# Pairs of heads on TensorE and half of the difference on ScalarE in the scan of the last two layers

## The reference, cut to what matters

```python
xbc = silu(causal_depthwise_conv(xbc, conv_w, conv_b))
xs, bm, cm = split(xbc, [1024, 1280])             # x, B and C
dt = softplus(dt_raw + dt_bias)                   # (256, 16)
A = -exp(a_log)                                   # (16,)
a_cs = cumsum(dt * A)                             # falls with t
decay[h, t, s] = exp(a_cs[t, h] - a_cs[s, h])     # for s <= t, else 0
y[t, h] = sum_s (C[t] . B[s]) * decay[h, t, s] * (x * dt)[s, h]   # B, C of the head's group
y = rmsnorm((y + d_skip * x) * silu(z), norm_w)
```

## Time and profile before

| | |
|---|---|
| median of 3 runs | 3577.18 us (3576.35 to 3582.57) |
| the profiled execution | 3575.29 us |
| its span, first to last instruction | 3573.5 us |
| TensorE (PE) busy | 3418.4 us, 96% |
| VectorE (DVE) busy | 1963.5 us, 55% |
| ScalarE (ACT) busy | 549.2 us, 15% |
| GpSimd (POOL) busy | 161.1 us, 5% |
| mean granted TensorE clock | 0.968 of full |

### The profile page before, as it was taken

How to read it: one execution, slowest core, us unless ns; L and a number is a source line. 1 busy time by engine, 2 the same in 40 slices (tenths; PEclk the granted TensorE clock), 3 DMA queues, 4 the chain that set the end, 5 groups by cost and what they waited for, 6 DMA issues and landing times. The chain is left out here.

```text
span 3573.5 us, 54659 instructions
## 1 busy us (share of the span) xinstructions
PE 3418.4 (96%) x23594; PEld 2873.7 (80%) x23594; DVE 1963.5 (55%) x2748; ACT 549.2 (15%) x1032; POOL 161.1 (5%) x166
## 2 busy tenths in 40 slices
PE   6999999997899989999899999999899999999999
PEld 2445475545788879998799999999888988889988
DVE  2266762225666746661566666644466665374772
ACT  1100011223343421001100000000101123101130
POOL 0000002000000010000000000000032000060000
PEclk7999999998889999999999999999999999999999
DMA  8887823102323244444344444455444433434423
GB/s 343 311 343 313 314 103 124 59 12 65 94 71 86 50 182 154 172 177 154 118 167 173 165 164 166 174 180 186 154 142 150 157 107 118 153 142 154 157 80 130
DMA packets 134896, 559.63 MB, mean 157 GB/s; under 512 B 57552, under 2 KB 61904, under 8 KB 72256
## 3 DMA queue, kind: packets, MB, share of 16 engines
q1 hardware_dynamic: 120256, 456.17, 36.3%
q10 hardware_dynamic: 14448, 100.62, 7.1%
HBM read 539.25 MB, written 17.30 MB: 156 GB/s over the span
## 5 line engine op out<-in xcount | busy, mean ns | idle before, releaser
L470 PE MATMUL ps<-arena,ring 128*128 128x256 f32 (+2 forms) x3168 | 829.6, 425 | 27.6 <-issue 11.8
L470 PEld LDWEIGHTS ps<-arena,ring 128*128 128x128 f32 x3168 | 609.0, 193 | 246.5 <-issue 172.6
L2586 PE MATMUL ps<-arena 128*128 128x128 f32 x2560 | 292.4, 275 | 0.0
L2586 PEld LDWEIGHTS ps<-arena 128*128 128x128 f32 x2560 | 289.1, 192 | 0.0
L2586 PE MATMUL ps<-arena,ring 128*128 128x128 f32 x1920 | 220.9, 275 | 0.0
L2586 PEld LDWEIGHTS ps<-arena,ring 128*128 128x128 f32 x1920 | 217.7, 192 | 0.1
L2992 PE MATMUL ps<-arena 128*128 128x128 f32 x1792 | 204.7, 275 | 0.0
L2992 PEld LDWEIGHTS ps<-arena 128*128 128x128 f32 x1792 | 202.4, 192 | 0.0
L801 DVE SCALAR_TENSOR_TENSOR arena<-arena,small 128x512 f32<-128x512 f32 x240 | 180.5, 752 | 37.3 <-DMA arena<-in_ada_late 21.3
L3545 PE MATMUL ps<-arena,ring 128*128 128x256 f32 x832 | 180.3, 379 | 0.0
L3545 PEld LDWEIGHTS ps<-arena,ring 128*128 128x128 f32 x832 | 157.9, 190 | 22.4 <-issue 1.0
(11 more groups left out here) (509 smaller groups left out, 4397.5 us busy)
## 6 DMA issues: line engine op xcount, KB each, us to landing
ring<-in_weights SPq DMA_DIRECT2D x402, 1024.0 KB, 4.8
arena<-in_ada_late ACTq DMA_DIRECT2D x64, 1024.0 KB, 8.9
arena<-in_gates SPq DMA_DIRECT2D x56, 256.0 KB, 3.5
arena<-in_front ACTq DMA_DIRECT2D x8, 1024.0 KB, 9.0
arena<-in_x ACTq DMA_DIRECT2D x2, 2048.0 KB, 12.7
keep_g<-arena SPq DMA_DIRECT2D x14, 256.0 KB, 2.0
arena<-keep_h SPq DMA_DIRECT2D x3, 1024.0 KB, 6.4
arena<-in_ctx ACTq DMA_DIRECT2D x1, 2048.0 KB, 23.8
```

The costliest lines, as they stand in the source:

```text
L470: mm = M.matmul(o, ring[:, slot, k, c0:c0 + w], rhs, start=(kc == 0), stop=(kc == ktiles * WK - 1))
L2586: mm = M.matmul(o, w[:, k], x(k), start=(k == 0), stop=(k == HD - 1))
```

## The change

The scan of both layers is done in another order and with another split of the work:

- Difference: VectorE makes only the first 256 columns, as max(sum - acs, 0), in one instruction, and no longer waits for its own end. The other 128 columns are made by ScalarE as Relu(sum - acs) (`later_half`), with a bias `acs_less`, which is -acs and is copied out of PSUM by one more small instruction of ScalarE (16 columns) in the projections.
- The sums have the opposite sign: `av` is dt * exp(a_log) and not its negative, and the exponential is taken with scale -1.
- `dd` and `dm` have four buffers instead of two, used by h % 4. VectorE runs difference(h + 2), weighing(h).
- TensorE takes the heads in pairs (`two_heads`): one wait for both, then the two even and odd matmuls of tau = 0, then the two of tau = 1, so that consecutive matmuls lie on different column halves of the array. Its order is sums(2), sums(3), and then sums(2q + 4), sums(2q + 5), pair q, for q = 0 to 5, then pairs 6 and 7.
- The sums from head 4 on wait for both VectorE's and ScalarE's part of the difference four heads before.
- ScalarE does an exp of two columns (`warm`) at the end of the projections, after its last silu.

```diff
@@ -2902,7 +2902,8 @@
         zdt, adt, dtv, av, acs = (view(28672 + 32 * n, 2, S_HEADS) for n in range(5))
         ea, lamv = view(28832, S_HEADS), view(28848, 8)
         cbm = view(28928, 2, 384)
-        dd, dm = view(29696, 2, 384), view(30464, 2, 384)
+        dd, dm = view(29696, 4, 384), view(31232, 4, 384)
+        acs_less = view(28864, S_HEADS)
         sqa = view(31232, 8, T)
         ys, sqs = view(33280, 8, T), view(35328, 8, T)
         cx, csq = view(33280, 4, T), view(34304, 4, T)
@@ -2915,7 +2916,7 @@
         N = {n: again(f"b2_{n}") for n in (
             "dt_mm z_in lnd dt_in a_in v_mm xs_mm cb_mm "
             "conv silu glu_s glu taps taps_pool ea "
-            "bc_mm diff dec dmul y_mm y_out v_in xs_in").split()}
+            "bc_mm diff relu dec dmul y_mm y_out v_in xs_in").split()}
 
         hX = view(16384, DC, T)
         dt_rows = sqa[:, 0]
@@ -3057,6 +3058,7 @@
 
             if h >= 4:
                 p.wait_ge(N['diff'].sem, N['diff'].due(p))
+                p.wait_ge(N['relu'].sem, N['relu'].due(p))
             M.matmul(ps[:, (h + 2) % 4, 0:T], av[:, 0, h:h + 1].to_broadcast([P, P]), C('upto', 2, T)[:, 0], start=True, stop=False)
             M.matmul(ps[:, (h + 2) % 4, P:T], av[:, 1, h:h + 1].to_broadcast([P, P]), C('upto', 2, T)[:, 1, P:T],
                      start=False, stop=True).then_inc(N['bc_mm'].sem, N['bc_mm'].up(p))
@@ -3064,12 +3066,8 @@
         def scan_diff(v, h):
 
             v.wait_ge(N['bc_mm'].sem, N['bc_mm'].due(v))
-            V.tensor_scalar(dd[:, h % 2, 0:T], ps[:, (h + 2) % 4, 0:T], acs[:, 0, h:h + 1], 0.0, ALU.subtract, ALU.min)\
-                .then_inc(dve_step.sem, dve_step.up(v))
-            V.tensor_scalar(dd[:, h % 2, T:T + P], ps[:, (h + 2) % 4, P:T], acs[:, 1, h:h + 1], 0.0, ALU.subtract, ALU.min)\
+            V.tensor_scalar(dd[:, h % 4, 0:T], ps[:, (h + 2) % 4, 0:T], acs[:, 0, h:h + 1], 0.0, ALU.subtract, ALU.max)\
                 .then_inc(N['diff'].sem, N['diff'].up(v))
-            v.wait_ge(dve_step.sem, dve_step.now(v))
-            v.wait_ge(N['diff'].sem, N['diff'].now(v))
 
         def mix_pe(p, l):
             block = lambda n, extra=None: column_block(p, mb, n % 2, 4, lambda kc: hB[:, kc, :], extra=extra)
@@ -3179,8 +3177,8 @@
             def drain_block(half, dst, extra=()):
 
                 a.wait_ge(mb.full[half].sem, mb.full[half].due(a))
-                for func, to, src in extra:
-                    S.activation(to, src, func).then_inc(act_step.sem, act_step.up(a))
+                for func, to, src, *factor in extra:
+                    S.activation(to, src, func, scale=factor[0] if factor else 1.0).then_inc(act_step.sem, act_step.up(a))
                 S.copy(dst, ps[:, 4 * half:4 * half + 4, 0:T]).then_inc(act_step.sem, act_step.up(a))
                 a.wait_ge(act_step.sem, act_step.now(a))
                 a.sem_inc(mb.free[half].sem, mb.free[half].up(a))
@@ -3223,6 +3221,7 @@
             S.activation(pj[:, 4:8], pj[:, 4:8], ACT.Sigmoid).then_inc(N['glu_s'].sem, N['glu_s'].up(a))
             for n in range(2, 6):
                 drain_block(n % 2, chunk4(n), [(ACT.Copy, acs[:], ps[:, 4, T:T + 32].rearrange("p (a b) -> p a b", a=2)),
+                                               (ACT.Copy, acs_less, ps[:, 4, T + 16:T + 32], -1.0),
                                                (ACT.Exp, lamv[:, 2:4], ps[:, 5, T:T + 2])] if n == 3 else ())
             S.activation(sqa[:, 0:4], qk[:, 0:4], ACT.Square).then_inc(at['sq'].sem, at['sq'].up(a))
             for c in XORD:
@@ -3265,6 +3264,8 @@
             S.copy(vT[:], ps[:, 2:4, :]).then_inc(N['v_in'].sem, N['v_in'].up(a))
             projected(11)
             silu(44, 4)
+            S.activation(warm, K('gate_b', 0, 2), ACT.Exp, scale=0.0).then_inc(act_step.sem, act_step.up(a))
+            a.wait_ge(act_step.sem, act_step.now(a))
 
         def cfm_taps(eng, step, E, l, chunks):
             for c in chunks:
@@ -3324,7 +3325,7 @@
             V.scalar_tensor_tensor(dtv[:], zdt[:], 0.0, adt[:], ALU.max, ALU.add)\
                 .then_inc(dve_step.sem, dve_step.up(v))
             v.wait_ge(dve_step.sem, dve_step.now(v))
-            V.scalar_tensor_tensor(av[:], dtv[:], -1.0, over(ea, 2, S_HEADS), ALU.mult, ALU.mult)\
+            V.scalar_tensor_tensor(av[:], dtv[:], 1.0, over(ea, 2, S_HEADS), ALU.mult, ALU.mult)\
                 .then_inc(N['a_in'].sem, N['a_in'].up(v))
             v.wait_ge(N['a_in'].sem, N['a_in'].now(v))
 
@@ -3425,19 +3426,23 @@
 
         def ssd_pe(p):
             p.wait_ge(N['xs_in'].sem, N['xs_in'].due(p))
-            def head(h):
-                c, e = h // 2, 64 * (h % 2)
-                p.wait_ge(N['dmul'].sem, N['dmul'].due(p))
-                o = ps[e:e + 64, 4 + c // 2, (c % 2) * T:(c % 2 + 1) * T]
-                M.matmul(o, xdt[:, 0, h], dm[:, h % 2, 0:T], start=True, stop=False)
-                mm = M.matmul(o[:, P:T], xdt[:, 1, h], dm[:, h % 2, T:T + P], start=False, stop=True)
-                mm.then_inc(N['y_mm'].sem, N['y_mm'].up(p))
-            for h in range(S_HEADS):
-                if h >= 2:
-                    scan_sums(p, h)
-                    head(h - 2)
-            head(14)
-            head(15)
+            def two_heads(q):
+                p.wait_ge(N['dmul'].sem, N['dmul'].due(p, 2))
+                for tau, lo, hi in ((0, 0, T), (1, T, T + P)):
+                    for h in (2 * q, 2 * q + 1):
+                        c, e = h // 2, 64 * (h % 2)
+                        o = ps[e:e + 64, 4 + c // 2, (c % 2) * T:(c % 2 + 1) * T]
+                        mm = M.matmul(o if tau == 0 else o[:, P:T], xdt[:, tau, h], dm[:, h % 4, lo:hi],
+                                      start=(tau == 0), stop=(tau == 1))
+                mm.then_inc(N['y_mm'].sem, N['y_mm'].up(p, 2))
+            scan_sums(p, 2)
+            scan_sums(p, 3)
+            for q in range(S_HEADS // 2):
+                if q < S_HEADS // 2 - 2:
+                    scan_sums(p, 2 * q + 4)
+                    scan_sums(p, 2 * q + 5)
+                two_heads(q)
+            p.wait_ge(N['relu'].sem, N['relu'].due(p, 4))
             p.wait_ge(N['diff'].sem, N['diff'].due(p, 4))
 
         y_read, piece_done, piece_in2 = again("y_read"), again("piece_done"), again("piece_in2")
@@ -3454,9 +3459,16 @@
         rms_s = rms(ys, 8, T, 1024, sqs, rs_s, bank=7)
 
         def ssd_act(a, l):
+            def later_half(h):
+                a.wait_ge(N['diff'].sem, N['diff'].due(a))
+                S.activation(dd[:, h % 4, T:T + P], ps[:, (h + 2) % 4, P:T], ACT.Relu, bias=acs_less[:, h:h + 1])\
+                    .then_inc(N['relu'].sem, N['relu'].up(a))
+            later_half(0)
             for h in range(S_HEADS):
-                a.wait_ge(N['diff'].sem, N['diff'].due(a))
-                S.activation(dd[:, h % 2], dd[:, h % 2], ACT.Exp).then_inc(N['dec'].sem, N['dec'].up(a))
+                if h + 1 < S_HEADS:
+                    later_half(h + 1)
+                a.wait_ge(N['relu'].sem, N['relu'].due(a))
+                S.activation(dd[:, h % 4], dd[:, h % 4], ACT.Exp, scale=-1.0).then_inc(N['dec'].sem, N['dec'].up(a))
             piece_copies(a, l, 0)
             a.wait_ge(N['y_out'].sem, N['y_out'].due(a))
             rms_s[1](a, root=False)
@@ -3464,21 +3476,19 @@
         def ssd_dve(v, l):
             def weigh(h):
                 v.wait_ge(N['dec'].sem, N['dec'].due(v))
-                if h >= 2:
+                if h >= 4:
                     v.wait_ge(N['y_mm'].sem, N['y_mm'].due(v))
-                V.tensor_tensor(dm[:, h % 2], dd[:, h % 2], cbm[:, h // 8], ALU.mult)\
+                V.tensor_tensor(dm[:, h % 4], dd[:, h % 4], cbm[:, h // 8], ALU.mult)\
                     .then_inc(N['dmul'].sem, N['dmul'].up(v))
                 v.wait_ge(N['dmul'].sem, N['dmul'].now(v))
             for h in range(S_HEADS):
-                if h >= 2:
-                    scan_diff(v, h)
-                if h >= 1:
-                    weigh(h - 1)
-            weigh(15)
+                if h + 2 < S_HEADS:
+                    scan_diff(v, h + 2)
+                weigh(h)
 
             V.tensor_tensor(yv[:, 8:12], cx[:], pj[:, 40:44], ALU.mult).then_inc(dve_step.sem, dve_step.up(v))
             v.wait_ge(dve_step.sem, dve_step.now(v))
-            v.wait_ge(N['y_mm'].sem, N['y_mm'].due(v, 2))
+            v.wait_ge(N['y_mm'].sem, N['y_mm'].due(v, 4))
             for c in range(8):
                 V.scalar_tensor_tensor(ys[:, c], xc[:, c], K2(l, 's_d', c),
                                                         ps[:, 4 + c // 2, (c % 2) * T:(c % 2 + 1) * T],
```

## The result

The changed kernel takes 3552.71 us in the median of 5 runs (3550.70 to 3562.66), against 3577.18 of the kernel before. The ratio is 0.9936, with a 95% interval of 0.9922 to 0.9951, so it is faster by 17.5 to 28 us. The gain was forecast at 18.8 us and came out at 24.5.

A forecast was written before the change was run, and what follows sets the result against it. TensorE's own work was taken to fill the scan's 1.64 us a head. Gains of 8.6 us in each layer's scan plus 1.6 for the clock, 18.8 in all, took 3577.2 to 3558.4 us, range 3555 to 3566.

The forecast's parts named there:

- The pace of TensorE before: Scan before the change: TensorE's own work fills the 1.64 us a head, 0.65 and 0.64 streaming, 0.35 changing shape.
- The two changes of shape: TensorE in the scan: some 0.20 us from head to sums and 0.15 from sums to head.
- the 1.8 us allowed below the forecast: Both scans: gain if the change to half shape costs nothing, 6 pairs a layer at 0.15 us each.
- The heads side by side: A pair's two heads on TensorE stream on both column halves at once, 0.64 us a pair, 0.76 as upper bound.
- The rival of heads in series: Halves do not overlap: heads cost 1.28 us, a pair 2.94, total 3565.9 us; chance 0.11.
- The others keep up: In the scan VectorE needs 2.0 to 2.2 us a pair, ScalarE 1.6 to 2.1, so TensorE is the bound at 2.30.
- The rival of the exchange: VectorE-ScalarE exchange becomes the scan's bound: 2.6 us a pair, 2.1 us lost a layer, 3562.6 us; chance 0.11.
- Start and tail: Layer 1's scan: pair 0 starts at 3421.0, the scores at 3436.47 instead of 3445.04, 8.6 us less.
- The clock in layer 0: Clock fall on layer 0's first two heads goes with about half the idle time: 1.6 us won, bounds 0 and 1.6.
- Table loads: ScalarE in the scan: no load expected, as Relu is in every table set; chance of loads 0.03.
- The rival on the slower side: Relu and exp alternate table loads on ScalarE: 3.37 us a head, 55 us later in both layers, 3632; chance 0.03.
- its own lower bound of 3556.6: Whole kernel: low end of the forecast's own range, 3558.4 us with 1.8 down for a free change to half shape.

The follow-up runs named there:

- e6: Changed kernel with TensorE taking single heads again, ScalarE's part and four buffers kept: 3567.07 us, ratio 0.9974.
- e3: Changed kernel with both heads of a pair on the same column half, one after the other, half the scan's output lost: 3566.98 us, ratio 0.9964.
- e5: Changed kernel with the second half of the difference back on VectorE, ScalarE with its exps alone, pairs and four buffers kept: 3569.4 us, ratio 0.9978.
- e7: Changed kernel with the sums of heads 4 and 5 behind pair 0 instead of ahead of it: 3560.94 us, ratio 0.9963.
- e9: Changed kernel without the early exp of two columns (`warm`): 3556.99 us, ratio 0.9949.
- e8: Changed kernel with scores of attention heads 0 and 1 between the last pairs, first outputs earlier, convolution product on GpSimd, exp(14) before Relu(15): 3561.77 us, ratio 0.9949.
- e11: The kernel with scores between the last pairs, run again unaltered beside a set of the changed kernel: 3556.21 us, ratio 0.9949.
- e4: Changed kernel with a pair's matmuls issued one head after the other, each head on its own column half: 3554.26 us, ratio 0.9927.

## Why the prediction missed its range

What was right, by its steps:

- The pace of TensorE before: streaming and changes of shape, 1.64 us a head. Shown by e6, where the others have slack and the pace stays. The two changes of shape were exchanged: by the rows it used, from head to sums is 0.79 less 0.64, 0.15 us, and from sums to head 0.85 less 0.65, 0.20 us. The 0.35 us a head stay, so the sum does too; only the 1.8 us allowed below the forecast, for a free change to half shape, would have been 2.4 (12 times 0.20).
- The heads side by side, 0.64 us a pair: 0.80 us up to the sums, and e3 puts a price of 0.64 on the halves. The rival of heads in series falls, and with it, for column halves and these matmuls, the Trainium skill's rule (TensorE: Matmul & The Clock Gate, Part 3) that weight loads overlap only where the row group differs.
- The others keep up, TensorE is the bound at 2.30 us a pair: 2.30 measured, VectorE waiting 0.37. e5 shows that this needs ScalarE's part. The rival of the exchange falls: ScalarE waits 0.54 us for a difference.
- Start and tail: pair 0 at 4.32 us behind the transposes (forecast 4.42), the scores at 19.75 (forecast 19.9).
- The clock in layer 0: right in direction, too large by 0.35 us. 1.6 us were forecast, and 9.96 less 8.71 is 1.25 us between the layers' gains. The 4.87 us for two heads less 3.28 is 1.59 us, but the whole scan was only 29.71 less 28.46, 1.25 us, longer. That the shorter idle stretch is the reason is supported by e7 and not shown (e5).
- Table loads: none in the scan of the changed kernel, and one for the whole scan in e9. The rival on the slower side falls.

That the scans' sum came within 0.13 us (18.67 against 18.8) is partly luck: the clock's term was 0.35 us too large, and the rest of each scan gave 0.11 us more than 8.6.

Sized wrongly, without effect: Relu takes 0.37 us and not 0.27. The next exp starts 0.27 us behind it all the same, so a head takes ScalarE 0.78 us from the Relu's start to the exp's end, near the forecast's 0.80. And the idle stretch ahead of pair 0 is 0.67 us and not about 1.0.

What failed is the last step, from the sum to the range. The sum put whatever the clock does outside the scans at nothing without a reason, and the range went only 1.6 us below its own lower bound of 3556.6, as "a little more for the spread of a median: 3555", a size taken from no row. In the two profiled spans the code outside the scans gave 3.9 us, and the medians of the three sets of the changed kernel are 3552.71, 3555.38 and 3554.16. Two things were missing.

First, a term outside the scans: 1.45 us between them and 0.19 behind them. The 1.45 us are a fall of the clock behind a wait of 2.12 us in layer 1's projections. It is in both profiles of the kernel before and in none of three of the changed one, but in one of two of the kernel with the scores between, so it is not shown to be an effect of the change. The clock in the trace of before showed this fall too, at 3136.7 us, but I looked at the clock in the scans alone. With it the difference is 9.96 + 8.71 + 1.45 + 0.19 = 20.3 us, and 3577.2 - 20.3 = 3556.9 would still have been above the measured median.

Second, the scatter of executions, much larger than I allowed. One kernel starts its first scan anywhere from 2921.6 to 2931.2 us, and its 21 runs lie between 3545.6 and 3567.8; the three runs shown of before (3576.35 to 3582.57) hid this. The median of those 21 runs is 3553.99 and their mean 3555.1; the standard error of the mean (how far a mean of so many runs would move if they were taken again) is 1.2 us, from their spread. So the 3552.71 of the first five is a low draw in part, and the second set's 3555.38 would have lain inside the range. Against 82 runs of the kernel before (mean 3577.4, standard error 0.6) the gain is 22.3 us, give or take 1.3; by the three sets, 23.4, 22.2 and 20.7. That is 2.0 us, some 1.5 errors, more than the 20.3 us that the profiles account for, and 3.4 us, some 2.6 errors, more than the 18.9 without the fall between the scans. Whether something lies behind these 2.0 to 3.4 us stays open: no profile shows it, and the runs do not settle it.

What makes the stretch ahead of the first scan vary stays open too. The clock's falls alone do not account for it: the two profiles of the kernel with the scores between have a mean granted clock of 0.96 there, both of them, and their first scans start 12.9 us apart.

Open as well is why the wait of 2.12 us is followed by a fall in some profiles and not in others. Its length is not what decides, since it is the same in all thirteen, and neither is the kernel alone, since e8 and e11 differ. That it depends on the instant at which the wait comes is an argument and was not tried.

## What to carry to other kernels

When TensorE's small matmuls alternate with full ones, count the changes of shape (here 0.15 us to the full shape and 0.20 back) beside the columns, group the small ones on different column parts, and check that the engines that feed them can follow the new pace: with either one left out, 3.3 to 3.5 of 8.7 us remained. Work that is ready can stand in an idle stretch of TensorE even if it isn't urgent: here that was worth 1.52 us a scan by itself, and it may spare a fall of the clock. A difference between two stages without a fall of the clock is good to hundredths of a microsecond where totals scatter by 20 us; a fall can add 1.25 to 1.7 us to any stage, so read the granted clock of every stage, and of more than one execution. And the range for a total must come from many executions, not from three.

## What the runs showed of the hardware

- Two column halves of the array run side by side wherever the matmuls stand within the group: 0.80 us for eight passes in turn, the same with one head behind the other (e4, 0.04 us a scan), 1.44 us on one half (e3).
- The clock's fall is worth 1.25 to 1.7 us a time here (1.25 by layer 0's scan against layer 1's in the kernel before, 1.43 in e7, 1.68 between e8 and e11), and equal waits have different ends: 1.98 us of idle time in e7 brought it in layer 0, and its twin in layer 1 did not; the same in the kernel before. 2.36 us of idle time in layer 0 of e5 brought none.
- Relu from PSUM with a bias for each partition, 128x128, takes 0.37 us, with 0.27 from its start to that of the next exp, and it needed no table load in either of the tables that were in place (e9).
